# Two transformer blocks on one core: norms and stage ends worked in halves of the tokens

## The reference

```python
def _rms_norm(x, g):
    return x * lax.rsqrt(jnp.mean(x * x, axis=-1, keepdims=True) + EPS) * g

# first model, two layers
h = _rms_norm(x, in_norm_g[l])
...                                   # mLSTM, HGRN2 and sliding-window attention from h @ w_in[l]
x = x + jnp.concatenate([m_out, h_out, s_out], axis=-1) @ w_out[l]
u = _rms_norm(x, mlp_norm_g[l]) @ w_up[l]
x = x + jnp.square(jax.nn.relu(u)) @ w_down[l]
gate = jax.nn.sigmoid(_rms_norm(x, ple_norm_g[l]) @ w_ple_gate[l])
x = x + gate * _rms_norm(p[l] @ w_ple_proj[l], ple_post_norm_g[l])

# second model, two layers; the shifts, scales and gates come from sc @ w_mod
h = rmsnorm(x, g_attn[layer]) * (1.0 + scale1) + shift1
x = x + gate1 * mixer_layer(h, w_in[layer], w_out[layer], ...)
h = rmsnorm(x, g_mlp[layer]) * (1.0 + scale2) + shift2
u, g = split(h @ w_up[layer])
x = x + gate2 * ((silu(causal_conv(g)) * u) @ w_down[layer])
return rmsnorm(x, g_final)
```

## Time and profile before

| | |
|---|---|
| time, median of 3 runs | 2976.93 us (2964.42, 2977.48, 2976.93) |
| the profiled execution | 2967.56 us, its span 2965.6 us |
| PE | 2811.8 us busy, 95% of the span |
| DVE | 1599.9 us, 54% |
| ACT | 1127.7 us, 38% |
| POOL | 208.9 us, 7% |
| DMA | 278.80 MB moved, mean 94 GB/s |
| mean granted clock of PE | 0.963 of full speed |

### The profile page before, as it was taken

The page is one execution under the profiler, slowest core; times in us unless marked ns, Lnnn a source line. Parts: engine busy times, 40 slices in busy tenths (PEclk is TensorE's granted clock), DMA queues, the critical chain, the costliest instruction groups (busy, mean ns, idle before and its releaser), DMA issues. The chain is left out here.

```text
span 2965.6 us, 37025 instructions
## 1 busy us (share of the span) xinstructions
PE 2811.8 (95%) x14756; PEld 2334.9 (79%) x14756; DVE 1599.9 (54%) x2673; ACT 1127.7 (38%) x1712; POOL 208.9 (7%) x224
## 2 busy tenths in 40 slices
PE   6998899999899889999989999899998999899998
PEld 5877788888788667888878878788887887788887
DVE  5744576555765548656576434553444534454443
ACT  6444332323554533322354444432323344332232
POOL 1311100001221210000120000100000000100001
PEclk9987999999999799999999999999998999999999
DMA  4210154443221014444422111223223211122321
GB/s 158 72 43 29 50 185 172 154 168 116 101 80 58 15 64 166 148 170 144 168 84 90 57 33 36 80 91 109 89 78 107 72 42 31 57 100 79 114 82 68
DMA packets 42979, 278.80 MB, mean 94 GB/s; under 512 B 6073, under 2 KB 6457, under 8 KB 11705
## 3 DMA queue, kind: packets, MB, share of 16 engines
q1 hardware_dynamic: 42808, 276.44, 26.7%
HBM read 274.33 MB, written 2.10 MB: 93 GB/s over the span
## 5 line engine op out<-in xcount | busy, mean ns | idle before, releaser
L306 DVE TENSOR_TENSOR low_panels<-raw_panels,high_panels 128x2048 fp32r<-128x2048 f32 (+3 forms) x218 | 469.5, 2154 | 339.2 <-ACT high_panels L293 339.0
L293 ACT ACTIVATE high_panels<-raw_panels 128x2048 fp32r<-128x2048 f32 (+3 forms) x218 | 392.6, 1802 | 469.8 <-PE bank L1527 147.8
L424 PE MATMUL bank<-mlp_h_high,high_panels 128*128 128x512 f32 x1152 | 451.5, 392 | 0.0
L424 PE MATMUL bank<-mlp_h_high,low_panels 128*128 128x512 f32 x1152 | 450.2, 391 | 0.0
L424 PE MATMUL bank<-mlp_h_low,high_panels 128*128 128x512 f32 x1152 | 448.8, 390 | 0.0
L424 PEld LDWEIGHTS bank<-mlp_h_high,low_panels 128*128 128x128 f32 x1152 | 216.3, 188 | 46.0
L424 PEld LDWEIGHTS bank<-mlp_h_low,high_panels 128*128 128x128 f32 x1152 | 216.3, 188 | 45.8
L424 PEld LDWEIGHTS bank<-mlp_h_high,high_panels 128*128 128x128 f32 x1152 | 216.4, 188 | 44.3
L449 PE MATMUL bank<-high_panels,h_high 128*128 128x256 f32 x704 | 208.2, 296 | 0.5 <-ACT values_and_ones L2039 0.5
L424 PE MATMUL bank<-h_high,high_panels 128*128 128x512 f32 x496 | 202.8, 409 | 1.8 <-DVE h_low L1409 1.6
L1527 PE MATMUL bank<-mlp_hid_high,high_panels 128*128 128x512 f32 x512 | 201.8, 394 | 0.0
(11 more groups left out here) (341 smaller groups left out, 5096.0 us busy)
## 6 DMA issues: line engine op xcount, KB each, us to landing
raw_panels<-in_w SPq DMA_DIRECT2D x236, 1024.0 KB, 4.8
raw_panels<-in_w SPq DMA_DIRECT2D x16, 384.0 KB, 3.1
raw_panels<-in_w SPq DMA_DIRECT2D x4, 960.0 KB, 4.7
raw_panels<-in_w SPq DMA_DIRECT2D x4, 768.0 KB, 4.2
row<-in_row SPq DMA_DIRECT2D x2, 1220.0 KB, 6.1
x<-in_xT SPq DMA_DIRECT2D x2, 1024.0 KB, 6.2
raw_panels<-in_w SPq DMA_DIRECT2D x4, 512.0 KB, 3.5
mix<-in_rope SPq DMA_DIRECT2D x2, 1024.0 KB, 6.3
```

The lines of the kernel that those rows point to most:

```text
L293: self.nc.scalar.activation(self.g.high[:, j % SPLIT, 0:raw.shape[1]], raw, ACT.Copy).then_inc(self.high_ready, 1)
L306: self.nc.vector.tensor_tensor(self.g.low[:, j % SPLIT, 0:w], raw, self.g.high[:, j % SPLIT, 0:w].bitcast(F32), ALU.subtract).then_inc(sel ...
L424: ins = nc.tensor.matmul(bank[:, :], w[a][:, k, c0:c0 + P], rhs[b][:, k0 + k, :], start=first and k == 0 and j == 0, stop=last and k == kt ...
```

## The change

1. A norm is worked per half of the tokens (`HalfNorm`): squares, total, root, spread, scale, rounding and rest are each done for 256 tokens, half a first, then half b.
2. In `layer_one` and `layer_two` the last eight groups (the second half of `w_out`) become 16 units, all eight chunks for half a, then all eight for half b, each with 256-wide matmuls. In `embedding_gate` the last four groups, and in `mlp_two` the last two, become such units as well. While the units of half b run, the norm of half a is finished and 5 (after `layer_one`), 4 (`embedding_gate`), 3 (`layer_two`) or 2 (`mlp_two`) chunks of the next stage's input are made.
3. The first four groups of the following stage are done in the order: groups 0 and 1 for half a, 2 and 3 for half a, 0 and 1 for half b, 2 and 3 for half b (`head_tensor`). The sums and the spread of half b stand between them. The second panel of a stage is no longer split at the end of the stage before, but in the head, behind half a's chunks.
4. `hh` and `hl` are one pair of buffers for all stages. The final norm is halved too, and leaves in pairs of half chunks.
5. The stage from `mlp_one` to `embedding_gate` keeps its whole norm.

```diff
+    def sum(self, pe, late=False):
+        added = self.direct[0] - self.first
+        if not late:
+            pe.wait_ge(self.on("added"), added)
+        for t in self.tiles:
+            self.nc.tensor.matmul(self.bank[:, t:t + 1], self.g.rstd[:, 1, t * P:(t + 1) * P], self.g.ones[:, 0:1], start=t == self.tiles[0], stop=False)
+        for i, c in enumerate(self.direct):
+            pe.wait_ge(self.on("squared"), i + 1 if late else added + i + 1)
+            for t in self.tiles:
+                ins = self.nc.tensor.matmul(self.bank[:, t:t + 1], self.g.sq[:, c % 2, t * P:(t + 1) * P], self.g.ones[:, 0:1],
+                                            start=False, stop=c == DC - 1 and t == self.tiles[-1])
+        ins.then_inc(self.on("summed"), 1)
...
+def head_norms(nc, g, s, name, c0, bank, gain, shift=None):
+    na = HalfNorm(nc, g, s, name + "_a", 0, g.bank[0], gain, shift, c0=c0)
+    nb = HalfNorm(nc, g, s, name + "_b", 1, bank, gain, shift, direct=(DC - 2, DC - 1))
+    return na, nb
...
+    def products(n, k, w, i, bank):
+        for j, (a, b) in enumerate(((0, 0), (0, 1), (1, 0))):
+            ins = nc.tensor.matmul(bank[:, n.cols], w[a][:, k, (i % 2) * P:(i % 2 + 1) * P], (g.hh, g.hl)[b][:, k, n.cols],
+                                   start=k == 0 and j == 0, stop=k == DC - 1 and j == 2)
+        return ins
+    if known:
+        na.spread(pe)
+        nb.spread(pe)
+    w = pan.parts(pe, first)
+    for k in range(DC):
+        if k == DC // 2 and not known:
+            nb.sum(pe, late=True)
+        na.made(pe, k)
+        for i in range(2):
+            products(na, k, w, i, banks[i])
+    if not known:
+        nb.spread(pe)
+    v = pan.parts(pe, first + 1)
+    for i in range(2, 4):
+        for k in range(DC):
+            products(na, k, v, i, banks[i])
+    for k in range(DC):
+        nb.made(pe, k)
+        for i in range(2):
+            ins = products(nb, k, w, i, banks[i])
+            if k == DC - 1:
+                ins.then_inc(full, 1)
+    for i in range(2, 4):
+        for k in range(DC):
+            ins = products(nb, k, v, i, banks[i])
+        ins.then_inc(full, 1)
...
+def head_scalar(act, na, nb, pan, first, known=False):
+    if known:
+        na.root(act, known=True)
+        nb.root(act, known=True)
+    else:
+        nb.square(act, DC - 2, late=True)
+        nb.square(act, DC - 1, late=True)
+    for c in range(na.c0, DC):
+        na.high(act, c)
+    pan.high(act, first + 1)
+    if not known:
+        nb.root(act)
+    for c in range(DC):
+        nb.high(act, c)
...
+def head_vector(dve, na, nb, pan, first, known=False):
+    if known:
+        na.invert(dve)
+        nb.invert(dve)
+    for c in range(na.c0, DC + 1):
+        if c < DC:
+            na.scale(dve, c)
+        if c > na.c0:
+            na.low(dve, c - 1)
+    pan.low(dve, first + 1)
+    if not known:
+        nb.invert(dve)
+    for c in range(DC + 1):
+        if c < DC:
+            nb.scale(dve, c)
+        if c >= 1:
...
+                def second(u):
+                    z, c = units[u]
+                    p = pan.parts(pe, 14 + c // 4)
+                    if u == 4:
+                        pe.wait_ge(x_updated, DC)
+                    if u >= len(unit_bank):
+                        pe.wait_ge(x_updated, DC + u - len(unit_bank) + 1)
+                    cols = slice(z * HALF, (z + 1) * HALF)
+                    for k in range(4, DC):
+                        if u == 0:
+                            pe.wait_ge(chunk_low, chunk_at[k] + 1)
+                        for j, (a_, b_) in enumerate(((0, 0), (0, 1), (1, 0))):
+                            ins = nc.tensor.matmul(unit_bank[u % len(unit_bank)][:, cols], p[a_][:, k - 4, (c % 4) * P:(c % 4 + 1) * P], (hh, hl)[b_][:, k, cols],
+                                                   start=k == 4 and j == 0, stop=k == DC - 1 and j == 2)
                     ins.then_inc(full, 1)
...
                         turn_chunk(c)
-                for i in second_groups:
-                    dense(i)
-                sum_partitions(nc, pe, g, nx)
+                for u in range(2 * DC):
+                    second(u)
+                    if u == DC + 1:
+                        xa.sum(pe)
+                    if u == DC + 3:
+                        xa.spread(pe)
...
-                for i in second_groups:
-                    evict(i)
+                pan.low(dve, 16)
+                for u in range(2 * DC):
+                    if u == DC + 3:
+                        xa.invert(dve)
+                    second(u)
+                    for i in made_behind.get(u, ()):
+                        xa.scale(dve, i)
+                        if i >= 1:
+                            xa.low(dve, i - 1)
+                    if u == DC + 6:
+                        xa.low(dve, MADE_LAYER1 - 1)
```

In `mlp_two` and `embedding_gate` the end of the stage on PE, and the final norm:

```diff
+    whole = DC - 2
+    calls = calls[:-4]
+    n_calls = len(calls)
+    units = [(z, part, c) for z in range(2) for part in range(2) for c in range(whole, DC)]
...
-                sum_partitions(nc, pe, g, nx)
+                for i, (z, part, c) in enumerate(units):
+                    w = pan.parts(pe, first + n_calls // 2 + part)
+                    j, cols = tail_slot(z, c), slice(z * HALF, (z + 1) * HALF)
+                    if part == 0:
+                        grp.free(pe, j)
+                    for k in range(rows[part]):
+                        for q, (a_, b_) in enumerate(((0, 0), (0, 1), (1, 0))):
+                            ins = nc.tensor.matmul(grp.bank(g, j)[:, cols], w[a_][:, k, (c % 2) * P:(c % 2 + 1) * P], (uh, ul)[b_][:, part * DC + k, cols],
+                                                   start=part == 0 and k == 0 and q == 0, stop=part == 1 and k == rows[1] - 1 and q == 2)
+                    ins.then_inc(full, 1)
+                    if i == 4:
+                        xa.sum(pe)
+                    if i == 5:
+                        xa.spread(pe)
...
+                for c in range(whole, DC):
+                    tail_update(0, c)
+                xa.invert(dve)
+                for c in range(MADE_MLP2):
+                    xa.scale(dve, c, None if y is None else y[:, c, :])
+                    if y is None and c >= 1:
+                        xa.low(dve, c - 1)
+                for c in range(whole, DC):
+                    tail_update(1, c)
+                if y is None:
+                    xa.low(dve, MADE_MLP2 - 1)
...
             def _(act):
-                root_of_mean(nc, act, g, e)
+                nz.square(act, DC - 2, late=True)
+                nz.square(act, DC - 1, late=True)
+                nz.root(act)
             @block.tensor
             def _(pe):
-                spread_rstd(nc, pe, g, e)
+                nz.sum(pe, late=True)
+                nz.spread(pe)
             @block.vector
             def _(dve):
-                invert_root(nc, dve, g, e)
+                for c in range(MADE_MLP2, DC):
+                    na.scale(dve, c, y[:, c, :])
+                nz.invert(dve)
                 for c in range(DC):
-                    nc.vector.scalar_tensor_tensor(y[:, c, :], x[:, c, :], gfin[:, c:c + 1], g.bank[0][:, :], ALU.mult, ALU.mult).then_inc(e.h_ready, 1)
+                    nz.scale(dve, c, y[:, c, :])
             @block.sync
             def _(sp):
-                for c in range(DC):
-                    sp.wait_ge(e.h_ready, c + 1)
-                    sp.dma_start(yT[:, c, :], y[:, c, :]).then_inc(s("stored"), 16)
+                for n in (na, nz):
+                    for c in range(0, DC, 2):
+                        if c + 2 > n.c0:
+                            sp.wait_ge(n.on("scaled"), c + 2 - n.c0)
+                        sp.dma_start(yT[:, c:c + 2, n.cols], y[:, c:c + 2, n.cols]).then_inc(s("stored"), 16)
...
+    units = [(None, c) for c in range(whole)] + [(z, c) for z in range(2) for c in range(whole, DC)]
+    n_units = len(units)
+    grp = Groups(["emb"] * DC + ["gate"] * n_units, {"emb": s("emb_kept"), "gate": s("gate_kept")})
...
-                sum_partitions(nc, pe, g, nx)
+                    if u == n_units - 4:
+                        xa.sum(pe)
+                    if u == n_units - 3:
+                        xa.spread(pe)
```

More of the change, by code:

```diff
@@ L1671, in _ @@
                 clear(pool, used)
-                add_squares(nc, pool, g, nx)
+                add_squares(nc, pool, g, nx, whole)
+                for c in range(whole, DC - 1):
+                    xa.add(pool, c)
+                for c in range(whole, DC - 2):
+                    xz.add(pool, c)
             @block.scalar
```

436 lines of the change are left out of this document (306 added, 130 removed).

## The result

The changed kernel takes 3003.57 us (median of four runs, 2996.20 to 3008.97), the kernel before, run beside it, 2970.94 (also four runs). The ratio is 1.0115, with a 95% interval of 1.0097 to 1.0134: slower by 33 us, where 30 us less were forecast.

A forecast was written before the change was run, and what follows sets the result against it. PE, busy 95%, bounds the kernel, so only its waits and half clock can be won: 107 us of loss become 82, 25 gained; final norm 3.5 and start 0.5 make about 30. Forecast 2944 us, range 2922 to 2968.

The forecast's parts named there:

- One buffer for `hh` and `hl` costs nothing: what it overwrites has been read.: All stages: sharing one pair of h buffers was priced at no cost.
- What halving costs on PE.: 1428 512-wide matmuls become 2856 of 256, 0.113 us each: priced at nothing, bounds 0 and 3 us.
- the rival: Halved matmuls: second weight loads not hidden, a further 0.113 us for each of 1428, 3105 us; chance 0.02.
- Of 6.9 us of cover 1.4 remain.: Layer one: ACT's chain to the levels starts 5.5 us later yet stays covered; otherwise up to 3 us lost per layer.
- My closing list: Signs of being wrong: layer one's first levels wait for the chain, modulation waits recur, half clock mostly over 5 us.
- The gate: Embedding gate to next layer: 4.3 norm matmuls, 2.2 end wait, 1.6 head wait; 8.1 us, twice, against 16.2 and 16.6.
- The barriers: Stage ends, PE waiting for DVE: 2.6 us after layer one, 2.3 layer two, 2.2 gate, 1.3 MLP two.
- The modulation pair: MLP one: PE waits 2.4 us, twice, at the second pair of modulation matmuls; bounds 0 and 5.
- MLP two into layer two: This stage change: 4.3 norm matmuls, 1.3 end wait, 3.3 head wait; 8.9 us against 16.5.
- the final norm: After the last matmul: 11.9 us against 15.4, 3.5 gained.
- Layer two into its MLP: This stage change: 4.3 + 2.3 + 2.5 + 0.9 = 10.0 us, twice, against 12.3 and 12.1.
- half a fall for each wait: PE's clock after the new 1 to 3 us waits: 2 us per stage change, 14 in all; bounds 0 and 31.

The follow-up runs named there:

- e5: Kernel before with the changed kernel's one shared h buffer for all stages, nothing done in halves; 3000.6 us, ratio 1.0111.
- e6: Kernel before with one shared h buffer, padded by 160 bytes in front and 96 behind; 2973.2 us, ratio 1.0018.
- e7: Changed kernel with 160 bytes of padding in front of h and 96 behind; 2969.8 us, ratio 1.0008.
- e1: Changed kernel with 32 bytes of padding in front of h and 96 behind; 3001.5 us, ratio 1.0120.
- e3: Changed kernel with 96 bytes of padding in front of h and 32 behind; 2988.9 us, ratio 1.0070.
- e8: Changed kernel with 96 bytes of padding in front of h and 160 behind; 2975.7 us, ratio 1.0030.
- e12: Kernel before with 128 bytes of padding in front of everything; 2967.3 us, ratio 1.0004.
- e17: e14 with the split of the next stage's first panel moved behind the root of half a in the gate; 2967.9 us, ratio 0.9993.
- e14: e7 with the embedding scaled earlier and, in the gate's half units, ACT squaring the unit before the last; 2969.2 us, ratio 1.0000.

## Why the prediction was wrong

**"One buffer for `hh` and `hl` costs nothing: what it overwrites has been read."** This step failed, and with it the sign. I checked what the buffer must wait for and not its address. The term that I put at nothing measured +33 us (e5) and goes when the same buffer starts 160 bytes later (e6). The trace of before could not show it, since all these tensors lay at distances 0 and 64. The one hint was that products went at 0.229 in the first model, where I took my pace, and at 0.227 in the second (the windows above); I did not look there.

**What halving costs on PE.** Priced at 0, bounds 0 and 3 us. At the same places (e7) two half products take 2 x 0.1177 = 0.2354 us where one whole took 0.2290: 0.0064 for each of 1428, 9.1 us; PE's busy time rose by 9.5 from e6 to e7. (Of the 46.5 us that it rose with the change, the other 37 are the place: 2858.3 after, 2821.8 in e7.) The row that I took, 0.113 in the earlier trace rows, had the panel as the moving operand and `h` as weights, the other way round from the halved products. That the second weight loads are hidden is right: each half product has its own load, and 0.0064 us is what a pair costs, not 0.113. With it the rival falls for which the prediction named the Trainium skill's page "TensorE: Matmul & The Clock Gate", section "LDWEIGHTS".

**"Of 6.9 us of cover 1.4 remain."** I saw the chain and its 5.5 us delay (measured 5.4: ACT's first eviction at 47.19 in e6, 52.56 in e7), but read the cover where level 2 starts, at 83.01. The operand that was ready at 76.10 is that of level 1, whose products stand in the row at 74.97 directly behind those of level 0: the first started at 76.24. Cover was nil, and the delay showed in full: 5.8 us and 2.5 of half clock, in both layers, 16.6 us where I took 0. My closing list named this as what would make me wrong.

**The gate.** 8.1 us against 16.2 before, a gain of 6 each with the clock. It lost 2.4 and 4.6. I let the root and reciprocal of half a lie beside two units, and did not ask whether the additions ahead of them were done. DVE is far behind PE there: ACT had the first half unit's sigmoid at 777.7 and DVE took it up at 782.25 (e7), after a split of 2.28 and an operation of 1.78 that takes 0.75 alone. PE waits 6.7 us for the total (5.7 in the run as changed). I had written that this wait "must be gone".

**Right in kind and near in size.** The barriers: 2.6, 2.3, 2.2 and 1.3 forecast; 2.4, 2.5, 3.6 and 1.2 measured. The modulation pair: 2.4 forecast, 2.7 measured, but with the clock about 5. MLP two into layer two (-5.2 against -5.6) and the final norm (-3.0 against -3.5) gained about what the sum gave them. Layer two into its MLP gained more (-5.8 and -6.4, where the terms give -3.4 each); why is open. The waits for `low_panels` in the tails are gone.

So of 63 us between forecast (-30) and result (+33) 33 are the address and about 36 the chain and the gates (23.6 lost where 12.6 were to be gained); the other places came out some 5 us better together, the 9 us of the halved products included. Without the address the forecast was still 27 us too good (e7 against e6, by medians): I had summed what goes at each seam, and for the two places where a chain passes over the seam I priced the cover from a row beside the one that mattered.

## What to carry to other kernels

Moving a tensor is an edit like any other: before a buffer is shared or allocated elsewhere, write down its start against the start of whatever PE loads beside it, and compare the count of products in equal windows before explaining waits. Here no edit of the order was worth as much as these 33 us. When work is split into halves, look for the chain that hangs on the first complete group, and take its cover at the first instruction that uses it. Change placement with the rest held fixed modulo 256 bytes, or two effects are mixed, as in e1 to e3. And before a few us between two executions are put down to an edit, lay one over the other and look whether they arise where the edit is.

## What the hardware showed that I had not expected

- The pace of 512-wide fp32 products depends on the distance between moving operand and weights in the partition, modulo 256 bytes: 0.2267 to 0.2275 us at 0, 0.2289 to 0.2293 at 64, 0.2326 to 0.2343 at the other multiples of 32 that were tried, a spread of 3% (e1 to e8, e12). What stands behind it is not settled: no run separates the loading of weights from the streaming. The Trainium skill's page "SBUF — State Buffer", section "A bandwidth-pool intuition that's wrong (but worth ruling out)", gives the weight loads a second, independent read port and says nothing of placement. Read as no interaction between the two, it would have placement change nothing, and these runs differ.
- For 256-wide products the order is another: halves of `h` at 0.1198 (distance 0), 0.1177 (64), 0.1181 (160), 0.1154 (192), 0.1183 (224); with the panel moving and `h` as weights 0.1198, 0.1138 to 0.1160, 0.1199, 0.1172 and 0.1170. Distance is not all that counts for them: in e7 the gate's halves took 0.1147 in one layer and 0.1178 in the other. A place that suits one width does not suit the other: e7 beats e8 by 6 us although its 512-wide products are slower.
- A DVE operation with two inputs took 1.35 to 1.48 us beside POOL's addition and 0.42 alone (e17, e14), and ended 0.27 to 0.28 us after that addition both times, as if it had stood until the addition was done. How much of PE's wait in the gates this makes was not measured. The Trainium skill's "GPSIMD Engine Reference", section "Specifications", says that GpSimd shares its SBUF interfaces with VectorE, with contention from DVE instructions that have two SBUF inputs; the trace agrees.
- The clock after short waits: behind one of 2.76 us the granted clock was 0.61 over the next 4 us (in part the 1.2 GHz level), behind 5.78 us 0.51 (e7). I had priced half a fall for each wait. And behind waits of 0.73 and 0.57 us the same products ran at 1.00 in one execution and at 0.57 in another (e7, e17); each such fall is about 1.6 us. Executions of one kernel that take longer also show a lower mean clock (the kernel before: 2961.3 us at 0.965, 2974.6 at 0.960).
